# The same kernel with its on-chip buffers packed at other addresses: large buffers first, start granularity 64 bytes in place of 2,048

## The reference

```
mod = silu(c) @ w_ada + b_ada            # 2048 -> 6*2048, gives sh1, sc1, g1, sh2, sc2, g2
h   = rms_norm(x, g1n) * (1 + sc1) + sh1
proj = h @ w_in                          # 2048 -> 6144: q, k, v of 8 + 8 heads of width 128
na_o = rms_norm(neighbourhood_attention(q, k, v, rpb))       # 8 heads, 2-D window
da_o = rms_norm(differential_attention(q, k, v, t5, lam))    # 8 heads, softmax1 - lam*softmax2
x = x + g1 * (concat(na_o, da_o) @ w_out)
h2 = rms_norm(x, g2n) * (1 + sc2) + sh2
x = x + g2 * ((silu(h2 @ w_gate) * (h2 @ w_up)) @ w_down)    # 2048 -> 5632 -> 2048
out = rms_norm(x, final_g)
```

## Time and profile before

| | |
|---|---|
| median of 3 runs | 2433.23 us (2433.11 to 2434.58) |
| the profiled execution: its time, and its span | 2433.23 us, 2431.5 us |
| busy: TensorE matmul, TensorE weight load | 2342.4 us (96%), 1896.7 us (78%) |
| busy: VectorE, ScalarE, GpSimd | 1183.8, 692.4, 329.4 us (49%, 28%, 14%) |
| mean granted TensorE clock | 0.983 |
| moved by DMA | 326.82 MB, mean 134 GB/s |

### The profile page before, as it was taken

The page is one execution under the profiler, slowest core; times in us unless marked ns, Lnnn a source line. Parts: engine busy times, 40 slices in busy tenths (PEclk is TensorE's granted clock), DMA queues, the critical chain, the costliest instruction groups (busy, mean ns, idle before and its releaser), DMA issues.

```text
span 2431.5 us, 29861 instructions
## 1 busy us (share of the span) xinstructions
PE 2342.4 (96%) x10298; PEld 1896.7 (78%) x10298; DVE 1183.8 (49%) x1623; ACT 692.4 (28%) x961; POOL 329.4 (14%) x278
## 2 busy tenths in 40 slices
PE   6689999999999998999999999999999999999997
PEld 3468888777776787788888888888888888888885
DVE  6885666777778788422233222233222233222334
ACT  3133333445455222322222222222222222222221
POOL 8961222000003232000000000000000000000032
PEclk8899999999999999999999999999999999999998
DMA  9863666443332786222233222233232233223232
GB/s 335 291 205 122 196 179 206 145 155 127 112 136 103 275 291 210 70 100 91 89 95 108 96 100 98 79 96 110 95 103 95 82 95 108 99 92 102 81 99 106
DMA packets 95889, 326.82 MB, mean 134 GB/s; under 512 B 11737, under 2 KB 11881, under 8 KB 94833
## 3 DMA queue, kind: packets, MB, share of 16 engines
q1 hardware_dynamic: 92162, 314.62, 38.2%
q0 software_dynamic: 2688, 11.60, 2.3%
q10 hardware_dynamic: 1008, 0.21, 0.1%
HBM read 322.15 MB, written 4.24 MB: 134 GB/s over the span
## 4 chain that ended last, share of the span: by engine, by line
PE 90%; DVE 4%; POOL 3%; issue 1%; DMA 0%; ACT 0%; DVEq 0%; POOLq 0%; ACTq 0%
PE P L388 20%; PE P L390 19%; PE P L389 19%; PE T L388 9%; PE T L389 9%; PE T L390 9%; DVE att L933 2%; PE T L452 1%; PE S L433 1%; DVE W_lo L924 1%; PE O L464 1%; PE O L466 1%; PE O L465 1%; PE S L434 1%; PE S L435 1%
## 5 line engine op out<-in xcount | busy, mean ns | idle before, releaser
L924 DVE TENSOR_TENSOR W_lo<-raw,W_hi 128x1024 fp32r<-128x1024 f32 (+2 forms) x436 | 495.4, 1136 | 781.1 <-ACT W_hi L647 777.7
L388 PE MATMUL P<-H_hi,W_hi 128*128 128x512 f32 x2112 | 840.5, 398 | 8.1 <-DVE H_lo L1343 3.3
L390 PE MATMUL P<-H_hi,W_lo 128*128 128x512 f32 x2112 | 824.6, 390 | 0.0
L389 PE MATMUL P<-H_lo,W_hi 128*128 128x512 f32 x2112 | 824.3, 390 | 0.0
L647 ACT ACTIVATE W_hi<-raw 128x1024 fp32r<-128x1024 f32 (+2 forms) x436 | 424.2, 973 | 1111.5 <-PE P L390 617.5
L388 PEld LDWEIGHTS P<-H_hi,W_hi 128*128 128x128 f32 x2112 | 397.5, 188 | 105.8 <-issue 18.8
L390 PEld LDWEIGHTS P<-H_hi,W_lo 128*128 128x128 f32 x2112 | 397.4, 188 | 85.0
L389 PEld LDWEIGHTS P<-H_lo,W_hi 128*128 128x128 f32 x2112 | 397.9, 188 | 80.8 <-issue 1.9
L1485 POOL TENSOR_TENSOR sq<-X 128x512 f32 (+1 forms) x38 | 61.5, 1618 | 1616.4 <-DVE X L1272 1490.2
L390 PE MATMUL T<-F_hi,W_lo 128*128 128x512 f32 x704 | 273.9, 389 | 0.0
L389 PE MATMUL T<-F_lo,W_hi 128*128 128x512 f32 x704 | 273.9, 389 | 0.0
(11 more groups left out here) (187 smaller groups left out, 1740.3 us busy)
## 6 DMA issues: line engine op xcount, KB each, us to landing
raw<-in_w_gu SPq DMA_DIRECT2D x176, 512.0 KB, 3.2
att<-in_w_ada SPq DMA_DIRECT2D x120, 512.0 KB, 4.9
raw<-in_w_in SPq DMA_DIRECT2D x84, 512.0 KB, 4.2
adar<-in_w_ada SPq DMA_DIRECT2D x72, 512.0 KB, 3.9
raw<-in_w_down SPq DMA_DIRECT2D x64, 384.0 KB, 3.0
raw<-in_w_down SPq DMA_DIRECT2D x64, 320.0 KB, 2.8
raw<-in_w_out SPq DMA_DIRECT2D x32, 512.0 KB, 4.8
raw<-in_w_first SPq DMA_DIRECT2D x16, 384.0 KB, 5.6
```

The costliest lines, as they stand in the source:

```text
L388: pe.matmul(bank[:, :], wh, xh, start=start, stop=False)
L389: pe.matmul(bank[:, :], wh, xl, start=False, stop=False)
L390: return pe.matmul(bank[:, :], wl, xh, start=False, stop=stop)
L924: dve.tensor_tensor(lo[:, 0:cols], raw[:, raw_slot * PW:raw_slot * PW + cols], hi[:, 0:cols].bitcast(F32), ALU.subtract).then_inc(lo_done, 1)
```

## The change

Only the places of the SBUF tensors change. The small tensors (`ones` to `nmax`) move from ahead of the large ones to behind `rstd`, `lams` moves in among them, LINE goes from 2,048 to 64, and the pad ahead of `att` is made at least 16 floats long. No instruction, semaphore, loop, DMA or PSUM bank is touched, and each engine's list of instructions is in the same order and of the same shapes as before.

```diff
+        H_hi = sb("H_hi", KT * S, F32R)
+        H_lo = sb("H_lo", KT * S, F32R)
+        x_at = (nc.sbuf_base + 31) // 32 * 32
+        X = sb("X", KT * S)
+        W_hi = sb("W_hi", 2 * PW, F32R)
+        W_lo = sb("W_lo", 2 * PW, F32R)
+        raw_at = (nc.sbuf_base + 31) // 32 * 32
+        raw = sb("raw", RAW_A * PW)
...
+        rstd = sb("rstd", S)
         ones = sb("ones", P)
         ident = sb("ident", P)
...
+        lams = sb("lams", 4 * 64)
         ldot, lexp, nlam = sb("ldot", 2), sb("lexp", 2), sb("nlam", 1)
         rs, rr = sb("rs", 8), sb("rr", 8)
         nmax = sb("nmax", 8)
 
-        LINE = 2048
-
-        def line_up(name):
-            short = -((nc.sbuf_base + 31) // 32 * 32) % LINE
-            if short:
-                sb(name, short // 4)
-
-        line_up("line_pad")
-        H_hi = sb("H_hi", KT * S, F32R)
...
-        rstd = sb("rstd", S)
-
+        LINE = 64
+        sb("line_pad", (-((nc.sbuf_base + 31) // 32 * 32) % LINE) // 4 or 16)
         overlay = (nc.sbuf_base + 31) // 32 * 32
         assert overlay % LINE == 0 and x_at % LINE == 0
         att = sb("att", 8192)
...
         gf = sb("gf", 2 * S)
-        lams = sb("lams", 4 * 64)
```

More of the change, by code:

```diff
@@ L121, in layer @@
         rstd = sb("rstd", S)
+        ones = sb("ones", P)
+        ident = sb("ident", P)
+        modp = sb("modp", 6 * KT * 2)
+        mod = sb("mod", 6 * KT)
+        st = sb("st", 8)
+        bT = sb("bT", 6 * KT)
+        gn1, gn2, gfin = sb("gn1", KT), sb("gn2", KT), sb("gfin", KT)
+        gna, gsub = sb("gna", NAH), sb("gsub", 1)
+        s1, s2 = sb("s1", KT), sb("s2", KT)
+        eps, root_warm = sb("eps", 1), sb("root_warm", 1)
+        lams = sb("lams", 4 * 64)
+        ldot, lexp, nlam = sb("ldot", 2), sb("lexp", 2), sb("nlam", 1)
+        rs, rr = sb("rs", 8), sb("rr", 8)
+        nmax = sb("nmax", 8)
+        LINE = 64
+        sb("line_pad", (-((nc.sbuf_base + 31) // 32 * 32) % LINE) // 4 or 16)
         overlay = (nc.sbuf_base + 31) // 32 * 32
```

## The result

The changed kernel takes 2449.67 us (median of 4 runs, 2449.0 to 2450.47) against 2433.9 us before: ratio 1.006, 95% interval 1.0048 to 1.0072, or +15.8 us. Over all 23 executions of it that were timed the median is 2448.8 us (2446.6 to 2451.2), so the last microsecond of the 15.8 is not certain. The time lies in the stated range, but the likeliest case had been no change.

A forecast was written before the change was run, and what follows sets the result against it. Taken as bound by matmuls from 156 us on, and by VectorE, GpSimd and DMA work before. Matmuls, VectorE/ScalarE/GpSimd and DMA each added 0, giving 2433.2 us; range 2424 to 2452 us, no change at 0.58.

The forecast's parts named there:

- What bounds the kernel: Whole kernel: matmuls fill TensorE from 156 us on; before that VectorE, GpSimd and DMA are nearly full.
- Part 1, the moving side: Matmuls of lines 388 to 390: a shifted moving operand was taken to cost 0, bounds 0 to +129 us.
- the nearest row: Weight load of `ones`, 128 past a multiple of 2,048: 190 ns against 188 for W_hi, hidden; basis for taking 0.
- faster: Dots between 20 and 98 us: the common remainder was itself a cost; 7.3 us would go, 2426 us; chance 0.18.
- The sign set for a dearer moving operand: Matmuls between 1400 and 2400 us: fewer than 4390 in those 1000 us would show the moving operand costs more.
- the DMA rival: First stage, 20 to 98 us: DMA engines become the bound; typical 2445 us; chance 0.17.
- f: Growth factor on DMA packet time: taken near 1, so 0 us; 1.06 fills the engines, 2 costs +134 us.
- The stationary side: Weight loads: cost 0, since each could grow by some 38 ns hidden behind the matmul.
- Part 2, VectorE, ScalarE, GpSimd: Operand starts, VectorE and GpSimd work before 156 us: 0 taken, bounds -4.5 to +4.5 us with GpSimd.
- Part 3, DMA: Transfers to shifted destinations: packet time nearly unchanged and covered by slack, so 0 us; upper end +134 us.
- Moving operand: All 9120 matmuls: two columns more each off the boundary, +8 us, 2441 us; chance 0.07.

The follow-up runs named there:

- e3: Kernel before with the whole first area (H, X, W, raw, sums) 64 bytes lower, F left in place: 2440.72 us in one run.
- e5: Kernel before with W_hi and W_lo 64 bytes further, raw and what follows, overlay included, 128 further: 2481.79 us in one run.
- e6: Changed kernel with F_hi and F_lo alone 64 bytes further, so F minus W is 256: 2435.4 us, ratio 1.0000.
- e2: Kernel before with F_hi and F_lo alone 64 bytes further: 2440.26 us, ratio 1.0023.
- e7: Kernel before with F_hi and F_lo alone 128 bytes further: 2449.85 us, ratio 1.0065.
- e8: Kernel before with F_hi and F_lo alone 192 bytes further: 2448.44 us, ratio 1.0056.
- e12: Kernel before with the down projection reading F 4, 48, 160 and 240 bytes past the tile's start, writes unchanged: 2453.97 us in one run.
- e11: Kernel before with 128 bytes of pad ahead of ones, so ones and ident start on multiples of 256: 2432.55 us, ratio 0.9996.

## Why the prediction missed its likeliest case

*What bounds the kernel* held. From 156 us on the matmul rate is the time, and that is why 16 columns on a fifth of the matmuls show in full.

*Part 1, the moving side: 0 taken.* This is the step that failed. It should have been 2112 x 6.7 = 14.1 us, within the bounds of 0 and 129 us that were kept for it. It failed in its reasoning, too. It priced each operand by its own start, and took from "the nearest row" a case where a stationary operand was off its multiple; e3 and e5 show that an own start says nothing. The two rows that seemed to exclude a gain or a loss, H and F both at 389 ns in different areas, had the same distance to W, namely 0, so they could not show what a distance costs. Line 960 was blind in the same way: its four offsets are all multiples of 512, so all are 0 over 256. And the 2 ns of the row of `ones` did not come from its start: in the changed kernel `ones` is again 128 past a multiple of 256, `sq` has come to 128 too, and the load takes 188 ns:

```profile
L463 PEld LDWEIGHTS M<-sq,ones x16: 187/188/188, 496.7 to 796.1; 128*128 128x128 f32 x16
```

The table of starts already held the answer: the change leaves H minus W at 0 and takes F minus W from 0 to 192. I read those 192 bytes only as a possible gain, in the rival "faster". The sign set for a dearer moving operand, fewer than 4390 matmuls between 1400 and 2400 us, did show it (4370), but it was set too low for its own rival: two columns on each would have left some 4396. That the measured time lies in the stated range is luck: the upper end, 2452 us, was that of the DMA rival at f = 1.3, which did not happen.

*The stationary side: 0, or hidden up to 38 ns.* The weight loads themselves did not grow (188 ns). But moving W costs as much per matmul as moving F (e5), so their spare time is no cover: the price appears in the matmul. The Trainium skill, "SBUF — State Buffer", section "Who interferes with whom", gives TensorE two read ports, one for the moving operand and one for weight loads, and calls them independent. Here the time of a matmul depends on where its two operands lie to each other (e5, 396 ns for 389); whether the two reads get in each other's way or something else does it, no run shows.

*Part 2, VectorE, ScalarE, GpSimd: 0 within 4.5 us.* Right: line 953 at 677 to 694 ns with `bias` now 64 past a multiple of 256 (the test that line 960 was not), dots at 1428 for 1427, and e6 at 1.0000.

*Part 3, DMA: f near 1.* Right. q1's packets take 38.2% of 16 x 2445.3 us for 92162, so 162 ns for 161: f is 1.006. By the rule in the Trainium skill, "DMA: Bandwidth & Descriptors", section "How a descriptor splits into AXI transactions", it would be an estimated 1.02 to 1.03 for these starts; no such growth shows, though the page speaks of reads and the starts that moved here are those of writes. The share of 0.94 in the first stage became 0.96 without a wait.

*The rivals.* "Moving operand" had the right place and side, with a chance of 0.07 that was far too low. Its condition was wrong (H is off its boundary too and costs nothing), and so was its size both ways: 2 columns on 9120 matmuls (8 us) for 16 on 2112. The DMA rival, with 0.17, took most of the weight given to slower and is shown wrong. "Faster" had the right thought, operands that walk through the same places together, but for VectorE's dots, which did not change; for matmuls the sign is the other one: a distance of 0 is the cheapest of the twelve tried.

*What stays open.* Why the distance matters and why 64 is cheap; which weights are the partner; and 1.7 us of the 15.8, since 14.1 are in the chunks. Against the median of all 23 executions it is 0.8 us. e2, e6, e7 and e8 also run 1.4 to 1.7 us behind before when they reach the first down projection, and the profiled run of the changed kernel is 0.4 us ahead there, so differences of this size come and go from run to run.

## What to carry to other kernels

When a change moves buffers, list the starts of the pairs that one instruction or two overlapping ones read together, and look at differences, not at each start. For float32 matmuls of 512 columns like these, keep the moving tiles and the weight blocks at the same place over 256 bytes; that gave the full rate with both at 0, at 128 and at 1,984 past a multiple of 2,048. Rounding the overlay to 128 in place of 64 repaired this kernel only because F then came to lie 256 bytes from W: a distance of 128 costs as much as one of 192 (e7). A row in which nothing differs in the quantity at issue is no evidence on its price.

## What the runs showed of the hardware that was not expected

- A float32 matmul of 512 columns starts every 226.7 ns when moving and stationary start differ by a multiple of 256 bytes, and 2.3 to 11.7 ns later at the eleven other distances tried. For 0, 64 and 192 this was the same with different starts of the two; the other nine were tried with one start of W.
- The same distance of 64, 128 or 192 in all three matmuls of a tile costs 16, 48 or 48 columns per tile (e2, e7, e8); 4 bytes cost most (e12).
- Transposes of 128 columns did not gain from a better place of `ident` (272 ns, e11), and VectorE, GpSimd and DMA showed no reaction to starts 64 or 128 past a multiple of 256 (GpSimd busy 69.57 for 70.72 us and VectorE 69.08 for 68.57 between 20 and 98 us, packets 162 for 161 ns).
